# Recurrent layer: the first five output products in three passes over split operands, outputs six steps behind their rows

## The reference

```python
zp = z @ w_in;  u, gate = split(zp)               # 2048 columns each
xc = conv_b + sum(up[:, tap:tap + T] * conv_w[tap] for tap in range(4))
y = lru_direction(xc, w_a[0], b_a[0], w_x[0], b_x[0], lam[0], reverse=False) \
  + lru_direction(xc, w_a[1], b_a[1], w_x[1], b_x[1], lam[1], reverse=True)
y = y * silu(gate)
return y @ w_out                                  # 2048 x 1024
# lru_direction: r, i = sigmoid(xc @ w_a + b_a), sigmoid(xc @ w_x + b_x), block diagonal (16 blocks of 128)
# a = exp(-8 r softplus(-lam));  b = sqrt(1 - a^2) i xc;  h_t = a_t h_(t-1) + b_t
```

## Time and profile before

| | |
|---|---|
| median of 3 runs | 1568.9 us (1567.67 to 1571.1) |
| profiled execution | 1567.02 us, span 1565.2 us |
| granted TensorE clock | 0.998 |
| busy: TensorE, VectorE, ScalarE | 1546.2, 1218.8, 891.2 us |
| line 2056 (16 outputs), first and last start | 362.2 and 479.5 us |

### The profile page before, as it was taken

How to read it: one execution, slowest core, us unless ns; L and a number is a source line. 1 busy time by engine, 2 the same in 40 slices (tenths; PEclk the granted TensorE clock), 3 DMA queues, 4 the chain that set the end, 5 groups by cost and what they waited for, 6 DMA issues and landing times.

```text
span 1565.2 us, 29418 instructions
## 1 busy us (share of the span) xinstructions
PE 1546.2 (99%) x10977; PEld 1441.4 (92%) x10977; DVE 1218.8 (78%) x1882; ACT 891.2 (57%) x1408; POOL 56.2 (4%) x70
## 2 busy tenths in 40 slices
PE   8999999999999999999999999999999999999998
PEld 8888889999889999999999999999999999999997
DVE  5866676778778877798778877888778787788776
ACT  5655565587784544486646444464445866464443
POOL 0000000000001000004000000000000030000000
PEclk9999999999999999999999999999999999999999
DMA  6553225455444655545565656556565654656552
GB/s 222 152 158 103 72 68 151 160 189 180 154 151 135 213 189 191 183 152 175 151 196 160 206 187 194 180 175 199 181 198 153 191 169 148 198 169 201 183 190 81
DMA packets 74289, 262.45 MB, mean 168 GB/s; under 512 B 8480, under 2 KB 10400, under 8 KB 74208
## 3 DMA queue, kind: packets, MB, share of 16 engines
q1 hardware_dynamic: 68352, 244.92, 49.6%
q0 software_dynamic: 3824, 14.05, 2.7%
q10 hardware_dynamic: 2032, 2.35, 0.6%
HBM read 258.16 MB, written 1.05 MB: 166 GB/s over the span
## 4 chain that ended last, share of the span: by engine, by line
PE 92%; DVE 3%; ACT 3%; issue 1%; ACTq 1%; DMA 1%; POOL 0%; DVEq 0%; POOLq 0%
PE PS L1779 19%; PE PS L1771 17%; PE PS L1773 16%; PE PS L1772 16%; PE PS L1780 10%; PE PS L2056 3%; PE PS L1987 1%; PE PS L2074 1%; PE PS L2226 1%; PE PS L1977 1%; PE PS L1966 1%; ACT w_hi L593 1%; PE PS L1963 1%; PE PS L1964 1%; PE PS L2215 0%
## 5 line engine op out<-in xcount | busy, mean ns | idle before, releaser
L1104 DVE TENSOR_TENSOR w_lo<-raw,w_hi 128x1024 fp32r<-128x1024 f32 x462 | 565.9, 1234 | 86.7 <-ACT w_hi L593 81.2
L593 ACT ACTIVATE w_hi<-raw 128x1024 fp32r<-128x1024 f32 x462 | 485.5, 1053 | 82.4 <-DMA raw<-stream 37.5
L1779 PE MATMUL PS<-Y,w_hi 128*128 128x512 f32 x1280 | 450.4, 393 | 0.0
L1771 PE MATMUL PS<-Y,w_hi 128*128 128x256 f32 (+1 forms) x1468 | 429.2, 292 | 3.8 <-DVE Y L1119 1.2
L1773 PE MATMUL PS<-Y,w_lo 128*128 128x256 f32 (+1 forms) x1468 | 416.8, 284 | 0.0
L1772 PE MATMUL PS<-Y,w_hi 128*128 128x256 f32 (+1 forms) x1468 | 416.3, 284 | 0.0
L1780 PE MATMUL PS<-Y,w_lo 128*128 128x256 f32 x1280 | 359.1, 281 | 0.0
L1779 PEld LDWEIGHTS PS<-Y,w_hi 128*128 128x128 f32 x1280 | 240.4, 188 | 51.4
L1771 PEld LDWEIGHTS PS<-Y,w_hi 128*128 128x128 f32 x1468 | 276.8, 189 | 10.4 <-issue 6.7
L1772 PEld LDWEIGHTS PS<-Y,w_hi 128*128 128x128 f32 x1468 | 276.3, 188 | 1.9 <-issue 0.5
L1773 PEld LDWEIGHTS PS<-Y,w_lo 128*128 128x128 f32 x1468 | 276.9, 189 | 0.0
(11 more groups left out here) (338 smaller groups left out, 1618.1 us busy)
## 6 DMA issues: line engine op xcount, KB each, us to landing
raw<-stream SPq DMA_DIRECT2D x462, 512.0 KB, 4.3
work<-stream POOLq DMA_DIRECT2D x24, 512.0 KB, 4.7
work<-work ACTq DMA_DIRECT2D x10, 136.0 KB, 3.6
X<-x SPq DMA_DIRECT2D x4, 272.0 KB, 3.4
out<-zf SPq DMA_DIRECT2D x3, 256.0 KB, 2.4
work<-work ACTq DMA_DIRECT2D x20, 34.0 KB, 2.4
work<-rope SPq DMA_DIRECT2D x1, 544.0 KB, 7.4
work<-levels POOLq DMA_DIRECT2D x1, 512.0 KB, 4.1
```

The source lines that it names most:

```text
L593: act.activation(w_hi[:, s.slot, :], raw[:, s.slot % RAW, :], ACT.Copy).then_inc(hi_ready, 1)
L1104: dve.tensor_tensor(w_lo[:, s.slot, :], raw[:, s.slot % RAW, :], f32(w_hi[:, s.slot, :]), ALU.subtract).then_inc(lo_ready, 1)
L1771: pe.matmul(to, wh, xh, start=start, stop=False, skip_group_check=True)
L1779: pe.matmul(both, wh, Y[:, :, k, 0:T2], start=start, stop=False, skip_group_check=True)
```

## The change

- `BEHIND` is 6: output 0 comes in step 6, output 8 in step 14, and outputs 9 to 15 after step 15. The bank plan of `odd_tiles` and the order of the whole slabs (`WHOLES`) follow from it.
- The first five outputs (`HALVED`) are three passes over split operands. ScalarE makes the high parts of slab and row (`output_high`), VectorE the low parts (`output_low`), for output k at the end of step k + 5. They lie in free rows of `Y` and in `hH`, `hL`, two of each. Per output: 24 fp32r matmuls of 256 columns in place of eight in fp32; two more ScalarE and two more VectorE instructions; four more semaphores. Outputs 5 to 15 stay fp32.

```diff
--- before.py
+++ after.py
@@ -76,7 +76,8 @@
 
 INPUTS_AT = {0: (4,), 1: (5,), 2: (6,), 3: (7, 8), 4: (9, 10), 5: (11,), 6: (12,), 7: (13,), 8: (14,), 9: (15,)}
 STEPS = 4 * GROUPS
-BEHIND = 5
+BEHIND = 6
+HALVED = 5
 
 SCANS_AT = {n: (n - 4,) for n in range(4, 13)}
 SCANS_AT.update({13: (9, 10), 14: (11,)})
@@ -295,6 +296,7 @@
         GR, GS = part(2, 4, T2), part(4, T2)
         WL = part(WHOLE, SLAB)
         HS = zf[:, 0:2, :]
+        OH, OL = ([y[:, DC + 4 * b:DC + 4 * b + 4, :].rearrange("p a t -> p (a t)")[:, 0:SLAB] for b in range(2)] for y in (YH, YL))
 
 
         taken[0] = 0
@@ -343,6 +345,7 @@
         sp_d, sp_a = sem("sp_d"), sem("sp_a")
         whole_landed, out_used = [sem(f"whole_landed{i}") for i in range(WHOLE)], sem("out_used")
         tap_done, xc_ready, lru_done, lru_out = sem("tap_done"), sem("xc_ready"), sem("lru_done"), sem("lru_out")
+        ow_hi, ow_lo, oy_hi, oy_lo = sem("ow_hi"), sem("ow_lo"), sem("oy_hi"), sem("oy_lo")
         gs_ready, gp_ready, li_ready, la_ready, tau_ready, sw_ready = sem("gs_ready"), sem("gp_ready"), sem("li_ready"), sem("la_ready"), sem("tau_ready"), sem("sw_ready")
         oy_ready = sem("oy_ready")
         fsig_ready, logsig_ready, mixf_ready = sem("fsig_ready"), sem("logsig_ready"), sem("mixf_ready")
@@ -1011,6 +1014,18 @@
                     act.wait_ge(tau_ready, 4 * g + 4)
                     act.activation(LW[:, g % 2], LW[:, g % 2], ACT.Sqrt, scale=0.25).then_inc(sw_ready, 1)
 
+                def output_high(k):
+
+                    i = WHOLES.index(("out", k))
+                    if k >= 2:
+                        act.wait_ge(out_used, k - 1)
+                    else:
+                        act.wait_ge(w_used, ring("u", 3).n + 1)
+                    act.wait_ge(whole_landed[i % WHOLE], 16 * (i // WHOLE + 1))
+                    act.activation(OH[k % 2], WL[:, i % WHOLE, :], ACT.Copy).then_inc(ow_hi, 1)
+                    act.wait_ge(oy_ready, k + 1)
+                    act.activation(hH[:, k % 2, 0:T2], GR[:, k // 4 % 2, k % 4, :], ACT.Copy).then_inc(oy_hi, 1)
+
                 def last_root(r):
                     act.wait_ge(tau_ready, 4 * LAST + r + 1)
                     lw = LW[:, LAST % 2, 2 * r:2 * r + 2, :]
@@ -1039,6 +1054,8 @@
                             split(ring("u", m).at(LEAD))
                         for m in inputs[1:]:
                             tap(*m)
+                        if 0 <= n + 1 - BEHIND < HALVED:
+                            output_high(n + 1 - BEHIND)
                         continue
                     if g and r == 1:
                         decay(g, 0)
@@ -1676,6 +1695,13 @@
                     dve.tensor_tensor(GR[:, gb, r, :], GR[:, gb, r, :], HS[:, 0, XO:], ALU.mult).then_inc(oy_ready, 1)
                     dve.wait_ge(oy_ready, n + 1)
 
+                def output_low(k):
+                    i = WHOLES.index(("out", k))
+                    dve.wait_ge(ow_hi, k + 1)
+                    dve.tensor_tensor(OL[k % 2], WL[:, i % WHOLE, :], f32(OH[k % 2]), ALU.subtract).then_inc(ow_lo, 1)
+                    dve.wait_ge(oy_hi, k + 1)
+                    dve.tensor_tensor(hL[:, k % 2, 0:T2], GR[:, k // 4 % 2, k % 4, :], f32(hH[:, k % 2, 0:T2]), ALU.subtract).then_inc(oy_lo, 1)
+
                 def token_factor(n):
 
                     dve.wait_ge(w_used, ring("u", n).n + 1)
@@ -1721,6 +1747,8 @@
                             split(ring("u", 4 * m[0] + m[1]).at(LEAD))
                         for m in inputs[1:]:
                             conv(*m)
+                    if 0 <= n + 1 - BEHIND < HALVED:
+                        output_low(n + 1 - BEHIND)
                 for r in range(4):
                     weighed(LAST, r)
                     scans(LAST, r)
@@ -2050,11 +2078,20 @@
 
                     w = whole("out", n)
                     pe.wait_ge(oy_ready, n + 1)
+                    if n < HALVED:
+                        pe.wait_ge(ow_lo, n + 1)
+                        pe.wait_ge(oy_lo, n + 1)
                     for m in range(DC):
                         if n == 0 and m % 2 == 0:
                             tile("out", 0, m // 2)
-                        last = pe.matmul(PS[:, m // 2, (m % 2) * T2:(m % 2 + 1) * T2], w[:, m * P:(m + 1) * P],
-                                         GR[:, n // 4 % 2, n % 4, :], start=n == 0 and m % 2 == 0, stop=n == 15, skip_group_check=True)
+                        to, ms = PS[:, m // 2, (m % 2) * T2:(m % 2 + 1) * T2], slice(m * P, (m + 1) * P)
+                        if n < HALVED:
+                            wh, wl, yh, yl = OH[n % 2][:, ms], OL[n % 2][:, ms], hH[:, n % 2, 0:T2], hL[:, n % 2, 0:T2]
+                            pe.matmul(to, wh, yh, start=n == 0 and m % 2 == 0, stop=False, skip_group_check=True)
+                            pe.matmul(to, wh, yl, start=False, stop=False, skip_group_check=True)
+                            last = pe.matmul(to, wl, yh, start=False, stop=False, skip_group_check=True)
+                        else:
+                            last = pe.matmul(to, w[:, ms], GR[:, n // 4 % 2, n % 4, :], start=False, stop=n == 15, skip_group_check=True)
                         if n == 15 and m in (1, 3, 5):
                             last.then_inc(sums_ready, 1)
                     last.then_inc(out_used, 1)
```

## The result

The changed kernel takes **1572.9 us** (median of 16 runs, 1571.7 to 1575.5) against 1568.5 us (16 runs, 1567.5 to 1571.3) for the kernel before on the same chip. The ratio is **1.0029, with a 95% interval of 1.0022 to 1.0035**: slower by 4.4 us, just past the 0.2% taken as the line. The profiled execution has a span of 1571.6 us.

A forecast was written before the change was run, and what follows sets the result against it. TensorE was busy 99%, but VectorE had almost no room where the first outputs run, so positions decided. Tail 28.8 less 26.0 us, gate 15 unmoved, gave +2.8 on the median 1568.9: 1571.7 us, range 1569.0 to 1576.0.

The forecast's parts named there:

- rival 2: VectorE becomes the bound of steps 7 to 10: +4.2 to +5.8 us, 1573.1 to 1574.7; chance 0.22.
- the likeliest case: The forecast itself, +2.8 us with 1 us to either side, 1570.7 to 1572.7; chance 0.48.
- my three outcomes: Verdicts against the 0.2% line of 3.1 us: same 0.49, slower 0.44, faster 0.07.
- Prices: Per split output: TensorE 2.8 us instead of 3.45, saving 0.65; VectorE 1.6 more, ScalarE 1.47 more.
- Steps 5 and 6: TensorE waits 1.6 us before gate 6, 1.9 before input 12, 0.8 before output 0; gate 7 starts at 376.9.
- Steps 7 to 9: Three outputs gain 1.95 us; VectorE's 10.2 just fits TensorE's 10.46 a step; 0.2 added for output 3.
- Step 10: Output 4 waits 3.4 us for its low parts queued behind scan 5, starting at 416.5; gate 11 at 419.3.
- Steps 11 to 15, tail: Gate 15 waits 1.4 us for gated(14), starting at 453.4 as before; tail takes 28.8 us instead of 26.0.
- Rival 3: Chain to gate 15 shortens to 13.4 from 14.8 us once VectorE catches up: +1.4, 1570.3; chance 0.23.
- Sum: By positions: tail 28.8 less 26.0 with gate 15 where it was, +2.8 us, 1571.7 on the median's scale.
- My second count, by waits: Over all waits: -3.25 work, new waits 1.6, 1.9, 0.8, 0.2, 2.3, 1.0, less 0.7 twice, makes +3.2 us.
- Rival 1: VectorE and ScalarE are ready when TensorE asks in steps 6 and 10: -5.7 us, 1563.2; chance 0.07.

The follow-up runs named there:

- fill: The changed kernel plus seven fp32 matmuls adding zero ahead of output 4's wait; ratio 1.0019 to the kernel before, +3.2 us.
- low_first: The changed kernel with VectorE's low parts of output k ahead of the scan of step k + 5 instead of behind it; 1567.67 us against 1568.06 before.
- passes_only: The changed kernel with the lag back at five steps (BEHIND 5), five three-pass outputs kept; ratio 1.0071 to the kernel before, +11.4 us.
- gate5_bank1: The changed kernel with gate 5 in bank 1 instead of bank 7; ratio 1.0030 to the kernel before, +5.1 us.
- scans_moved: The changed kernel with row 10 scanned in step 14 instead of 13; ratio 1.0024 to the kernel before, +3.6 us.
- row_high_later: The changed kernel at lag five, row's high part behind the next step's tanh, low parts behind the gate's split; ratio 1.0093 to the kernel before, +14.7 us.
- four: The changed kernel with four three-pass outputs instead of five, output 4 in one fp32 pass; ratio 1.0009 to the kernel before, +1.7 us.
- low_first_scans: The changed kernel with low parts ahead of the scan and row 10 scanned in step 14; 1566.13 us, ratio 0.9986 to the kernel before.

## Why the prediction came out as it did

The forecast was +2.8 us, 1571.7, with a band of 1570.7 to 1572.7; measured were +4.4 and 1572.9. The range holds it, with some luck: it reaches past 1572.7 only for rival 2, whose mechanism falls below, and for the measurement. It lies past the band of the likeliest case and on the other side of the 0.2% line: the more probable of my three outcomes was "same", and it is slower. The step that failed is the sum: it has a term for each wait and each instruction and none for what a 3 us wait does to the clock. "The granted clock is 1.00, so nothing here is about the clock" was right of the kernel before and was carried over to one in which I had just put a wait of 3.4 us. A slip in the chances besides: my four add up to 1, so the 0.1 outside the range for steps that go worse came from no case.

- **Prices.** Held. Output 1 starts at 385.87 and gate 8 at 388.68: 2.81 us, where I had 2.8. VectorE's two instructions take 1.22 and 0.42, ScalarE's 1.05 and 0.41. The tail, 484.89 - 456.15 = 28.74 for 28.8, says that the fp32 output costs 3.45. The Trainium skill (FP8 and Floating Point Precision, TensorE Precision Notes) gives four passes for a true fp32 product; my estimate from it, 32 fp32r matmuls for an output or an estimated 3.73 us, would have made the tail 30.7. The page states no time, so it is this estimate that the trace refutes, not the four passes.
- **Steps 5 and 6.** The three waits were placed rightly and are 1.34, 0.97 and 1.29 for 1.6, 1.9 and 0.8. Input 12 starts at 369.58 on the clock of the kernel before (370.69 less 1.11), 0.7 earlier than I had: ScalarE is done with that tanh sooner. Output 0 absorbs it here, since it waits for VectorE in any case: it starts at 374.16 for 374.1. Where several engines are late for one point, only the last matters, and that one was right. Small products of step 7 less 3.02 give gate 7: 376.9, as forecast.
- **Steps 7 to 9.** Outputs 1 and 2 don't wait. Output 3 starts 0.18 us after input 15's last matmul should end (407.02 for 406.71 + 0.13) and 0.15 after its low part (406.87), with no wait in brackets: the 0.2 that I had put behind ScalarE's square roots. The small products stand at 381.01, 391.49, 401.98 and 412.75, steps of 10.48, 10.49 and 10.77 for 10.46, 10.46 and 10.66. Rival 2 (VectorE becomes the bound) falls on this, although the time that it gave, 1573.1 to 1574.7, is nearest to the measured one: a time that fits is no evidence for a mechanism.
- **Step 10.** Place and cause held: 3.09 for 3.4, output 4 at 416.7 on the old clock for 416.5. Gate 11 should have started at 419.3 and started at 421.06. 1.4 of these 1.8 us are the clock, which fill shows by itself; 0.4 are the lateness of output 4 and of rounding.
- **Steps 11 to 15, tail.** From the small products of step 13 (441.32) to gate 15 are 14.83 us, for 14.8; the wait is 1.28 for 1.4. Rival 3 (that chain gets shorter) falls. Output 8 and the tail wait for no row, as told. But this chain starts from the small products of step 13, and they were not within 0.2 of 438.6: on the old clock they start at 440.21, 1.6 later, by the clock and the lateness of step 10. The chain handed that on in full, and gate 15 starts at 455.04 for 453.4.
- **Sum.** By positions, 4.29 in the layer = 2.8 + 1.4 + 0.1. My second count, by waits, does not close as well: 1.34, 0.97, 1.29, 3.09 and 1.28 are 8.0, less 2.9 before, less 3.25 of work, plus 1.4 is 3.2, about 1.1 short. The bracketed idle time is less than the gap between work: output 0 starts 1.45 us after input 12's last matmul should end (373.69 + 0.13) for 1.29 in brackets, the other gaps are 0.16 to 0.18 longer than their brackets too, and output 3's has none. That covers about half; the rest of the 1.1 I can't place.
- **Rival 1** (faster) asked that VectorE and ScalarE be ready in steps 6 and 10. I gave it 0.07, since nothing in the code as changed makes them so. low_first shows that the order of two calls does for step 10; step 6 still waits 1.34 and 1.08 there. The mechanism was real; the change did not set it off.
- **Bookkeeping.** VectorE is busy 7.4 us more for 8.2, ScalarE 5.9 for 7.4. The two added groups alone come to the forecast (5 x 1.64 and 5 x 1.46), so what is missing lies elsewhere in the trace; it carries no part of the argument.

## What to carry to other kernels

An added instruction costs what stands behind it in its engine's in-order queue, not what it takes: with the same ten VectorE instructions the kernel is 4.4 us slower than before where they stand behind a scan, and no slower where they stand ahead of it. Five waits of ScalarE's for a scan, with the next step's tanh behind them, came with 9.9 us of waits of TensorE in a kernel 11.4 slower. When a sum contains a wait of TensorE of 3 us or so where there was none, price what the clock does after it, or put work there. And when a wait is to be removed, look at who is late next: gate 6's wait was worth nothing; with output 4 back in one pass, its wait and the slow stretch gone, 2.7 of the 4.4 us were back.

## What was not expected of the hardware

- After waits of 2.93 and 3.21 (passes_only), 3.08 (gate5_bank1), 3.09 (the change), 3.10 (scans_moved), 3.79 and 4.10 us (row_high_later) the granted clock is 0.50 for a while; after waits of 1.3, 1.76 and 2.38 us (the change, four, low_first_scans) it stays 1.00. In the changed kernel it is still at 1.00 for the first 1.1 us of work after the wait, then at 0.50 for about 3.2 us, though TensorE is busy without a gap. There the matmuls that pay are not those that stand next to the wait: nine of output 4's run at full speed and fifteen do not.
- Where the slow stretch begins is not fixed. The same wait in scans_moved, in the same place of the same work, has it begin before the wait is over: the first matmuls already start 0.21 apart, and from 419.8 on the clock is back. In row_high_later it also begins within the wait and lasts longer, from about 366.2 to 373.0; by an estimate from the 25 starts that are 0.213 us apart it costs 2.4 us (25 x 0.096). Timelines of TensorE, scans_moved and then row_high_later:

```profile
416.90 0.55 PE L2090 MATMUL PS<-hH,Y 128*128 128x256 f32 x1 [3.10 <-DVE hL L1703]
```

```profile
367.54 0.42 PE L2095 MATMUL PS<-hL,Y 128*128 128x256 f32 x1
367.76 0.41 PE L2096 MATMUL PS<-hH,Y 128*128 128x256 f32 x1
```

- A full-precision product of 256 columns takes 3.45 / 8 = 0.431 us and three passes take 0.351. Three passes so save 19% of TensorE's time for such a product here, and each split output costs the other two engines 1.64 and 1.46 us.
